# Dilated attention: turning the probabilities by a product with a diagonal matrix of reciprocal sums instead of scaling and transposing them

## The chip, the cores and the metric

The kernel runs on one core of one Trainium2 chip. The metric is the device time of one execution in microseconds. The times shown are medians of several executions; the profile is one execution taken by the hardware profiler, whose own clock starts at the first instruction and ends at the last (the span).

## The reference, cut to what matters

The program is a deep block: two layers of feed-forward network, mixer, feed-forward network with layer norms, then two more layers of a second kind of mixer. Only the mixer of the second layer matters here, dilated attention over 512 positions with three groups (window 128 at stride 1, 512 at stride 4, 2048 at stride 16), 16 heads of 64 each:

```python
scores = einsum(q, k) * E ** -0.5 + bias          # bias: minus slope times distance
scores = where(valid, scores, MASK_VALUE)
lse = logsumexp(scores, axis=-1)
p = exp(scores - lse[..., None])
o = einsum(p, v)                                  # per group
...
wts = softmax(stack(lses), axis=0)                # over the three groups
o = sum(wts[..., None] * stack(outs), axis=0)
return o.reshape(B, S, ATTN_WIDTH) @ w_out
```

A softmax over groups, weighted by their log-sums, is one softmax over the keys of all three groups. So the kernel puts the scores of the three groups side by side (512 + 128 + 128 columns for 128 queries), takes one minimum, one exponential, one sum and one reciprocal per query and head.

## The kernel before, in words

The stages run one after another: start, feed-forward, pooling mixer, two feed-forwards, **dilated attention**, feed-forward, two mixers of the second kind, end. Every engine has its own program; they meet in semaphores (`s["..."]`). Activations lie feature by position, 8 tiles of 128 x 512.

SP loads weights in chunks, GpSimd (POOL in the profile) splits each chunk into a high and a low part (`pool_weights`, two operations at L337 and L339 of up to 2048 columns per partition), and TensorE (PE) multiplies with both (L358, L989).

The attention stage (`pe_attn`, `act_attn`, `dve_attn`) treats the 16 heads in four **quads** of four. For each quad come nine weight chunks for q, k and v of the three groups (18 half chunks), then eight **pairs** `i`. A pair is two heads (`hh` = 0, 1) and one residue `r` of the query position, that is 128 queries. Per pair the engines do, in the order in which their instructions are issued:

- **TensorE**, iteration i of a quad: `pe_attn_turn(i-1, 0)`, `pe_attn_turn(i-1, 1)`, `pe_attn_scores(i+1)` and `pe_attn_out(i-1)`, below T0, T1, S and O. A turn transposes the probabilities of one head, six blocks of 128 x 128 (four of the far group at L861, two of the near groups at L867), into PSUM. S is ten score products (L848): six of 512 columns and four of 128. O is twelve products of turned probabilities with values (L887). In iteration 8 there is no S, and in the first three quads a half chunk of the next quad (24 matmuls of 512 columns, L358) stands ahead of the last turn.
- **VectorE** (DVE), iteration i: far scores of head 0 (L912), reciprocal (L934) and scaling (L935) of head 1 of pair i-1, near scores of both heads (L921), far scores of head 1 (L912), two minima (L928), reciprocal and scaling of head 0 of pair i. After pair 5 a low part of the output is split off (L1033).
- **ScalarE** (ACT), iteration i: three copies of the turned probabilities from PSUM to `at_pt` (L895), two exponentials with the sum as by-product (L902). After pair 5 also the high part of the output.

The waits around the change: T0 and T1 wait for `normed`; T0 also for `pt_copied` of the pair before; a scaling waits for `probs`; the exponential of head `hh` waits for `t_done`, because it overwrites `at_pr`, which the turns read; S waits for `sc_ready` of the pair before (its scores taken out of PSUM); O waits for `pt_copied`; the first far scores of a pair wait for `scored`.

`nc.tensor.transpose(out, x, identity)` is a matrix instruction in transpose mode, with `x` as the stationary operand and the identity as the moving one. `nc.tensor.matmul(out, x, d)` computes x transposed times d.

Of the kernel before, what the change touches and what calls it, by code (L numbers as in the profile page):

```python
# [20 lines left out]
F32 = mybir.dt.float32  # L21
# [4 lines left out]
P = 128  # L26
T = 512
# [186 lines left out]
class Kernel:  # L214
# [45 lines left out]
    def sb(self, name, shape, dt=F32, ctx=None):  # L260
        return (ctx or self.ctx).enter_context(self.nc.sbuf_tensor(name, shape, dt))
# [542 lines left out]
    def memory_attn(self, own):  # L804
        sb = self.sb

        self.at_qk0 = sb("at_qk0", [P, 2, 2, T], F32R, own)
        self.at_qk0_l = sb("at_qk0_l", [P, 2, 2, T], F32R, own)
        self.at_q = sb("at_q", [P, 2, 2, T], F32, own)
        self.at_k = sb("at_k", [P, 2, 2, T], F32, own)  # L810
        self.at_v = sb("at_v", [P, 3, 4, 256], F32, own)
        self.dist0 = (self.sq, sb("dist0", [P, 2, T], F32, own))
        self.dist12 = sb("dist12", [P, 2, P], F32, own)
        self.at_oh = sb("at_oh", [P, KT, T], F32R, own)
        self.at_ol = sb("at_ol", [P, KT, T], F32R, own)
        self.at_bias = self.stats[:].rearrange("p a (b t) -> p (a b) t", b=2)
        self.at_sc, self.at_pr = (sb(n, [P, 2, T + 2 * P], F32, own) for n in ("at_sc", "at_pr"))
        self.at_pt = sb("at_pt", [P, 3, T], F32, own)
        self.at_nb, self.at_den, self.at_rd = (sb(n, [P, 2, 2], F32, own) for n in ("at_nb", "at_den", "at_rd"))

# [32 lines left out]
    def pe_attn_turn(self, pe, st, i, hh):  # L853
        nc, s, ps = self.nc, self.s, self.ps
        pe.wait_ge(s["normed"].sem, st.at("normed", 2 * i + hh + 1))
        if i and hh == 0:
            pe.wait_ge(s["pt_copied"].sem, st.at("pt_copied", 3 * i))

        def far():
            for j in range(4):  # L860
                mm = nc.tensor.transpose(ps[:, self.TURNED + 2 * hh, j * P:(j + 1) * P], self.at_pr[:, hh, j * P:(j + 1) * P], self.identity[:])  # L861
            s["t_done"].up(mm)

        def near():
            for g in range(2):
                at = hh * 2 * P + g * P
                mm = nc.tensor.transpose(ps[:, self.TURNED + 1, at:at + P], self.at_pr[:, hh, T + g * P:T + (g + 1) * P], self.identity[:])  # L867
            if hh:
                s["t_done"].up(mm)
        for step in ((near, far) if hh else (far, near)):  # L870
            step()
# [58 lines left out]
    def dve_attn_norm(self, dve, st, i, hh):  # L930
        nc, s = self.nc, self.s
        dve.wait_ge(s["probs"].sem, st.at("probs", 2 * i + hh + 1))
        rd, pr = self.at_rd[:, i % 2, hh:hh + 1], self.at_pr[:, hh]
        self.dve_then(dve, nc.vector.reciprocal(rd, self.at_den[:, i % 2, hh:hh + 1]))  # L934
        s["normed"].up(nc.vector.tensor_scalar(pr, pr, rd, None, ALU.mult))  # L935

    @staticmethod
    def by_residue(ap):
# [1412 lines left out]
```

## Time and profile before

| | |
|---|---|
| median of 3 runs | 3788.59 us (3788.31 to 3789.31) |
| the profiled execution's own time | 3787.25 us |
| its span, first to last instruction | 3785.4 us |
| TensorE busy | 3440.3 us, 91% |
| VectorE busy | 1737.8 us, 46% |
| ScalarE busy | 798.0 us, 21% |
| GpSimd busy | 2200.1 us, 58% |
| pairs of the attention stage | from about 1485 to 2006 us of the span, in four stretches of some 53 us |

How to read it: the shares are averages over stages with different limits. The pairs are four stretches of 1/18 of the span together, and the change touches nothing outside them; what matters is the order of events in them, which the rows below show.

### The profile page before, as it was taken

To read this page: it belongs to the slowest core of one execution; us is meant where nothing else is said; L and a number is where in the kernel's file an instruction comes from. 1 tells how busy PE (TensorE), PEld (TensorE's weight loads), DVE (VectorE), ACT (ScalarE), POOL (GpSimd) and SP (SyncE) were. 2 spreads that over 40 slices of the span, in tenths; PEclk is the share of its full clock that TensorE was granted. 3 is DMA by queue.
4 is the path that set the end of the run, shared out by engine and by line. 5 is a ranking of instruction groups with operands and counts; after the bars stand their busy time and mean duration, and the time that the engine had idled before them with its cause. 6 is when DMAs were issued, how large, how long until landed. Compare 5 with 4: busy or idle time off the path is not lost.

```text
span 3785.4 us, 42681 instructions
## 1 busy us (share of the span) xinstructions
PE 3440.3 (91%) x16956; PEld 2739.8 (72%) x16956; DVE 1737.8 (46%) x2017; ACT 798.0 (21%) x1345; POOL 2200.1 (58%) x558
## 2 busy tenths in 40 slices
PE   6999878999899979989897999868999987899997
PEld 5887656888688858778775888646678765667875
DVE  6772574222422242351536222365667525566742
ACT  1000212110211022231323110031322212132321
POOL 6776555777577746436353777635445663445564
PEclk9999989999899989999998999979999998999998
DMA  5553222323223222112121232212222221222221
GB/s 179 177 177 107 82 67 67 96 90 98 72 89 98 92 78 89 45 56 81 42 78 45 78 100 95 89 55 67 62 63 66 77 91 56 62 56 67 68 81 64
DMA packets 321300, 312.56 MB, mean 83 GB/s; under 512 B 11376, under 2 KB 303888, under 8 KB 320784
## 3 DMA queue, kind: packets, MB, share of 16 engines
q1 hardware_dynamic: 303840, 277.91, 23.7%
q10 hardware_dynamic: 17328, 32.80, 2.5%
q8 instruction: 94, 1.54, 0.2%
q14 instruction: 38, 0.31, 0.0%
HBM read 308.57 MB, written 2.10 MB: 82 GB/s over the span
## 4 chain that ended last, share of the span: by engine, by line
PE 74%; DVE 15%; ACT 5%; issue 4%; DMA 2%; ACTq 0%; DVEq 0%
PE ps L358 48%; PE ps L1229 12%; PE ps L989 4%; DVE sq L1110 2%; PE ps L1271 2%; PE ps L463 1%; DMA ada_raw<-in_ada_w 1%; ACT x L494 1%; PE ps L1796 1%; ACT xh L500 1%; DVE at_sc L912 1%; DVE score L1561 1%; DVE top L1560 1%; DVE d_pr L1650 1%; PE ps L1609 1%
## 5 line engine op out<-in xcount | busy, mean ns | idle before, releaser
L337 POOL TENSOR_TENSOR wh<-w_raw,zero 128x2048 fp32r<-128x2048 f32 (+2 forms) x277 | 952.4, 3438 | 1522.1 <-PE ps L358 1016.0
L339 POOL TENSOR_TENSOR wl<-w_raw,wh 128x2048 fp32r<-128x2048 f32 (+2 forms) x277 | 1247.6, 4504 | 21.7
L358 PE MATMUL ps<-xh,wh 128*128 128x512 f32 x2160 | 857.1, 397 | 101.7 <-DVE xl L536 48.0
L358 PE MATMUL ps<-xl,wh 128*128 128x512 f32 x2160 | 847.9, 393 | 0.0
L358 PE MATMUL ps<-xh,wl 128*128 128x512 f32 x2160 | 847.5, 392 | 0.0
L358 PEld LDWEIGHTS ps<-xh,wh 128*128 128x128 f32 x2160 | 409.3, 190 | 211.0 <-issue 91.9
L358 PEld LDWEIGHTS ps<-xh,wl 128*128 128x128 f32 x2160 | 409.7, 190 | 86.7
L358 PEld LDWEIGHTS ps<-xl,wh 128*128 128x128 f32 x2160 | 410.3, 190 | 83.0 <-issue 1.0
L1229 PE MATMUL ps<-xh,wh 128*128 128x512 f32 x688 | 294.0, 427 | 8.1 <-ACT stats L1371 6.4
L358 PE MATMUL ps<-hid_h,wh 128*128 128x512 f32 x704 | 279.7, 397 | 7.6 <-DVE mod L1125 7.6
L626 DVE TENSOR_TENSOR hp<-sg,ps 128x512 f32<-128x512 f32 x88 | 60.3, 685 | 481.2 <-PE ps L358 481.2
L358 PE MATMUL ps<-hid_l,wh 128*128 128x512 f32 x704 | 279.4, 397 | 0.0
L358 PE MATMUL ps<-hid_h,wl 128*128 128x512 f32 x704 | 279.4, 397 | 0.0
L1229 PE MATMUL ps<-xl,wh 128*128 128x512 f32 x688 | 274.4, 399 | 0.0
L1229 PE MATMUL ps<-xh,wl 128*128 128x512 f32 x688 | 274.2, 399 | 0.0
L629 DVE TENSOR_TENSOR hid_l<-hp,hid_h 128x512 f32 x88 | 190.7, 2167 | 87.7 <-ACT hid_h L611 87.7
L640 DVE SCALAR_TENSOR_TENSOR x<-x,ps 128x512 f32<-128x512 f32 x32 | 22.0, 686 | 378.6 <-PE ps L358 378.6
L1229 PEld LDWEIGHTS ps<-xh,wh 128*128 128x128 f32 x688 | 132.9, 193 | 61.6 <-issue 31.5
L472 ACT ACTIVATE squares<-x 128x512 f32<-128x512 f32 x64 | 37.8, 626 | 654.2 <-DVE x L514 634.0
L358 PEld LDWEIGHTS ps<-hid_h,wh 128*128 128x128 f32 x704 | 132.9, 189 | 39.9 <-issue 7.7
L611 ACT ACTIVATE hid_h<-hp 128x512 f32 x88 | 55.6, 632 | 494.4 <-DVE hp L626 494.4
L358 PEld LDWEIGHTS ps<-hid_l,wh 128*128 128x128 f32 x704 | 133.0, 189 | 32.2
(286 smaller groups left out, 5102.0 us busy)
## 6 DMA issues: line engine op xcount, KB each, us to landing
w_raw<-in_w_in SPq DMA_DIRECT2D x120, 512.0 KB, 4.1
w_raw<-in_ffn_w_gate SPq DMA_DIRECT2D x88, 512.0 KB, 4.6
w_raw<-in_ffn_w_up SPq DMA_DIRECT2D x88, 512.0 KB, 4.8
w_raw<-in_attn_w_qkv SPq DMA_DIRECT2D x72, 512.0 KB, 4.5
w_raw<-in_ffn_w_down SPq DMA_DIRECT2D x64, 512.0 KB, 3.6
ada_raw<-in_ada_w ACTq DMA_DIRECT2D x24, 512.0 KB, 5.5
stats<-in_ada_w ACTq DMA_DIRECT2D x24, 512.0 KB, 5.1
w_raw<-in_ffn_w_down SPq DMA_DIRECT2D x32, 384.0 KB, 4.1
```

The lines of the kernel that those rows point to most:

```text
L337: t = s["w_hi"].up(pool.tensor_tensor(hi, raw, self.zero[:, 0:1].to_broadcast([P, n]), ALU.subtract))
L339: s["w_lo"].up(pool.tensor_tensor(lo, raw, hi.bitcast(F32), ALU.subtract))
L358: mm = self.nc.tensor.matmul(out, a[:, slot, w], b(t), start=start and t == 0 and q == 0, stop=stop and t == k - 1 and q == 2)
L463: s["var_part"].up(self.nc.tensor.matmul(self.ps[:, bank], self.ones[:], self.pair_at(p)[:], start=p == 0, stop=p == PAIRS - 1))
L494: t = s["x_ready"].up(nc.scalar.activation(self.x[:, m], self.x[:, m], ACT.Identity, scale=self.ln[:, 0, u, m:m + 1], bias=self.ln[:, 1, u ...
L611: s["hid_hi"].up(nc.scalar.activation(self.hid_h[:, 2 * i + m], self.hp[:, m], ACT.Copy))
L626: t = s["hid"].up(nc.vector.tensor_tensor(self.hp[:, m], self.sg[:, m], self.ps[:, 2 + m], ALU.mult))
L629: s["hid_lo"].up(nc.vector.tensor_tensor(self.hid_l[:, 2 * i + m], self.hp[:, m], self.hid_h[:, 2 * i + m].bitcast(F32), ALU.subtract))
L989: mm = self.nc.tensor.matmul(out, x[t][:, r], b[:, slot, w], start=t == 0 and q == 0, stop=t == KT - 1 and q == 2)
L1110: ins = v.scalar_tensor_tensor(total, raw, c, total, ALU.mult, ALU.add)
L1229: mm = self.nc.tensor.matmul(out, a[:, slot, w], b(t), start=first and t == ks[0] and q == 0, stop=last and t == ks[-1] and q == 2)
L1271: mm = self.nc.tensor.matmul(out, x[t][:, r], b[:, c % 2, w], start=t == 0 and q == 0, stop=t == KT - 1 and q == 2)
```

## The change

The scaling pass over 768 columns of probabilities (L935) goes. In its place VectorE scales the 128 x 128 identity by the reciprocal sums, row by row, which gives a diagonal matrix in a new tile `at_dg`. The six transposes of each head become six ordinary float32 products of the unscaled probabilities with that matrix: entry (k, q) of such a product is p(q, k) times 1/sum(q), so turning and scaling are one operation. The calls, their waits and their order stay the same.

```diff
+        self.at_dg = sb("at_dg", [P, 2, P], F32, own)
 ...
         def far():
             for j in range(4):
-                mm = nc.tensor.transpose(ps[:, self.TURNED + 2 * hh, j * P:(j + 1) * P], self.at_pr[:, hh, j * P:(j + 1) * P], self.identity[:])
+                mm = nc.tensor.matmul(ps[:, self.TURNED + 2 * hh, j * P:(j + 1) * P], self.at_pr[:, hh, j * P:(j + 1) * P], self.at_dg[:, hh], start=True, stop=True)
             s["t_done"].up(mm)
 
         def near():
             for g in range(2):
                 at = hh * 2 * P + g * P
-                mm = nc.tensor.transpose(ps[:, self.TURNED + 1, at:at + P], self.at_pr[:, hh, T + g * P:T + (g + 1) * P], self.identity[:])
+                mm = nc.tensor.matmul(ps[:, self.TURNED + 1, at:at + P], self.at_pr[:, hh, T + g * P:T + (g + 1) * P], self.at_dg[:, hh], start=True, stop=True)
             if hh:
                 s["t_done"].up(mm)
 ...
     def dve_attn_norm(self, dve, st, i, hh):
         nc, s = self.nc, self.s
         dve.wait_ge(s["probs"].sem, st.at("probs", 2 * i + hh + 1))
-        rd, pr = self.at_rd[:, i % 2, hh:hh + 1], self.at_pr[:, hh]
+        rd = self.at_rd[:, i % 2, hh:hh + 1]
         self.dve_then(dve, nc.vector.reciprocal(rd, self.at_den[:, i % 2, hh:hh + 1]))
-        s["normed"].up(nc.vector.tensor_scalar(pr, pr, rd, None, ALU.mult))
+        s["normed"].up(nc.vector.tensor_scalar(self.at_dg[:, hh], self.identity[:], rd, None, ALU.mult))
```

## Rows read from the trace of the kernel before

**Rows 1.** The page, the chain of work that ended last, by engine.

```profile
PE 74%; DVE 15%; ACT 5%; issue 4%; DMA 2%; ACTq 0%; DVEq 0%
```

**Rows 2.** Windows: length; busy (x) of PE, PEld, DVE, ACT, POOL; PEclk; DMA.

```profile
1671.49:1677.02 5.53, 4.64 (x53) 3.76 (x51) 5.19 (x10) 3.63 (x7) 0.00 (x0) 1.00 0.01 3
1655.50:1660.20 4.70, 4.65 (x28) 3.95 (x30) 4.39 (x7) 3.14 (x6) 0.00 (x0) 0.50 0.71 227
```

**Rows 3.** Timeline of VectorE, one pair of quad 2: start, length, operation, [idle before].

```profile
1670.29 0.62 DVE L935 TENSOR_SCALAR at_pr<-at_pr,at_rd 128x768 f32<-128x768 f32 x1
1670.83 0.74 DVE L912 SCALAR_TENSOR_TENSOR at_sc<-sq,slopes,ps 128x512 f32<-128x512 f32 x1
...
1672.81 0.74 DVE L912 SCALAR_TENSOR_TENSOR at_sc<-sq,slopes,ps 128x512 f32<-128x512 f32 x1
1673.58 1.81 DVE L928 TENSOR_REDUCE at_nb<-at_sc 128x1 f32<-128x768 f32 x2
1675.63 0.16 DVE L934 RECIPROCAL at_rd<-at_den 128x1 f32<-128x1 f32 x1 [0.24 <-ACT at_pr L902]
```

**Rows 4.** Timeline of TensorE in the same pair: first rows of T0, T1 and S.

```profile
1671.06 0.66 PE L861 MATMUL ps<-identity,at_pr 128*128 128x128 f32 x4
...
1672.35 0.44 PE L867 MATMUL ps<-identity,at_pr 128*128 128x128 f32 x2 [0.42 <-DVE at_pr L935]
...
1673.70 0.47 PE L848 MATMUL ps<-at_qk 64*128 64x512 f32 x1 [0.47 <-DVE at_sc L912]
```

**Rows 5.** Timeline of TensorE early in quad 2, one iteration in which it waits for nothing.

```profile
1661.34 0.66 PE L861 MATMUL ps<-identity,at_pr 128*128 128x128 f32 x4
...
1662.27 0.60 PE L861 MATMUL ps<-identity,at_pr 128*128 128x128 f32 x4
1662.80 0.50 PE L848 MATMUL ps<-at_qk 64*128 64x512 f32 x1
...
1664.27 1.53 PE L887 MATMUL ps<-at_pt,at_v 128*64 128x128 f32 x24
1665.73 0.44 PE L861 MATMUL ps<-identity,at_pr 128*128 128x128 f32 x2
```

**Rows 6.** VectorE scaling, lines of L935 and L1050: count, shortest/median/longest ns, first and last start.

```profile
L935 DVE TENSOR_SCALAR at_pr<-at_pr,at_rd x64: 619/621/4021, 1495.4 to 2002.2; 128x768 f32<-128x768 f32 x64
```

```profile
L1050 DVE TENSOR_SCALAR stats<-dist,slopes x32: 285/288/4661, 1413.7 to 1884.8; 128x128 f32<-128x128 f32 x32
```

**Rows 7.** TensorE, lines of L861 (transposes) and L1877 (plain products of another stage).

```profile
L861 PE MATMUL ps<-identity,at_pr x256: 270/273/474, 1496.4 to 2003.5; 128*128 128x128 f32 x128
```

```profile
L1877 PE MATMUL ps<-sd,gv x64: 271/275/275, 2911.1 to 3644.9; 128*128 128x128 f32 x64
```

**Rows 8.** Timeline of TensorE in the second kind of mixer.

```profile
2913.02 0.61 PE L1877 MATMUL ps<-sd,gv 128*128 128x128 f32 x4
```

**Rows 9.** Timeline of all engines, head of quad 2.

```profile
1650.38 4.70 POOL L339 TENSOR_TENSOR wl<-w_raw,wh 128x2048 fp32r<-128x2048 f32 x1
...
1651.48 4.01 DVE L935 TENSOR_SCALAR at_pr<-at_pr,at_rd 128x768 f32<-128x768 f32 x1
...
1655.55 0.69 PE L867 MATMUL ps<-identity,at_pr 128*128 128x128 f32 x2 [3.23 <-DVE at_pr L935]
```

**Rows 10.** Timeline of VectorE after pair 5 of quad 2.

```profile
1682.58 0.69 DVE L1033 TENSOR_TENSOR at_ol<-ps,at_oh 128x512 fp32r<-128x512 f32 x1 [0.58 <-ACT at_oh L1006]
```

**Rows 11.** Timeline of TensorE, end of quad 2: T0 of pair 6, O of pairs 6 and 7.

```profile
1688.93 0.65 PE L861 MATMUL ps<-identity,at_pr 128*128 128x128 f32 x4
...
1691.86 1.53 PE L887 MATMUL ps<-at_pt,at_v 128*64 128x128 f32 x24 [0.74 <-ACT at_pt L895]
...
1701.16 1.09 PE L887 MATMUL ps<-at_pt,at_v 128*64 128x128 f32 x16 [0.79 <-ACT at_pt L895]
```

**Rows 12.** Timeline, end of quad 4: T0 of pair 6, O of pair 7.

```profile
1996.53 0.66 PE L861 MATMUL ps<-identity,at_pr 128*128 128x128 f32 x4
...
2004.52 1.53 PE L887 MATMUL ps<-at_pt,at_v 128*64 128x128 f32 x24 [0.74 <-ACT at_pt L895]
```

## The prediction

> **What bounds the kernel now.** I read the page first, for the chain that ended last: it is TensorE's for the most part [rows 1], and the attention pairs are one place where that is not so. Then the timelines of the pairs, engine by engine, in a stretch without GpSimd or DMA traffic, and last the single lines for prices.
>
> In the steady part one pair follows another every 5.53 us, from one reciprocal of head 1 to the next, at the full clock of 2.4 GHz (PEclk 1.00), and VectorE is busy for 5.19 of them [rows 2]. Its one gap is 0.24 us, in which the reciprocal of head 0 waits for the exponential [rows 3]. TensorE waits twice in the same pair: T1 for the scaling of head 1, 0.42 us, and S for the far scores of head 1, 0.47 us [rows 4]. So VectorE, with the short ScalarE step in its loop, sets the pace. But TensorE is not far behind: early in a quad, where it has a backlog, one iteration takes 1.46 us for T0 and T1 (1661.34 to 1662.80), 1.47 for S and 1.46 for O (1664.27 to 1665.73), 4.39 us in all [rows 5]. The reader should see both numbers, 5.54 and 4.39: the change takes from the first and adds to the second.
>
> At the head of a quad something else holds: the scaling of head 1 of the first pair takes 4.01 us instead of 0.62, because it started inside a 4.70 us operation of GpSimd (1650.38 to 1655.08) and ended 0.41 us after it; T1 waited 3.23 us for it [rows 9]. In that gap the granted clock had fallen to 0.50, that is 1.2 GHz, and it stayed there over the whole of 1655.5 to 1660.2 although TensorE was busy for 4.65 of those 4.70 us [rows 2].
>
> **Change, VectorE's part.** Removed per head: a pass over 768 columns, 0.62 us long (median 621 ns), after which the next operation starts 0.54 us later [rows 3, 6]. Added: the same operation on 128 columns of an SBUF tile; L1050 is just that, 288 ns [rows 6]. So each head gives VectorE 0.33 us and each pair 0.67: its loop could turn in 5.54 - 0.67 = 4.87 us. At the head of a quad the short operation still can't start before GpSimd is through (the longest L1050 took 4661 ns [rows 6]); only the 0.41 us behind GpSimd's end shrinks, to about 0.08, so T1 starts 0.33 us earlier, at about 1655.2.
>
> **Change, TensorE's part.** A transpose is one matrix instruction: 64 heads x 4 at L861 give x256 records. A plain float32 product is two: L1877 issues 32 of them (two mixers, four heads, four blocks) and has x64 records of the same length, 271 to 275 ns [rows 7]. The step from one record to the next is what occupies the engine. For four transposes in a row it is (0.60 - 0.27)/3 = 0.11 us [rows 5]; for two plain products of 128 x 128 by 128 columns, four records, it is (0.61 - 0.275)/3 = 0.11 us as well [rows 8]. So a turned block costs 0.11 us now and 0.22 after. Bounds: 0.11 if the product with the diagonal were as cheap as a transpose, for which no row speaks; 0.23 if each pair of records lost a little to the doubled weight loads. I take 0.22, from the operation of the same shape and type. Twelve blocks per pair: T0 and T1 grow by 1.32 us, from 1.46 to 2.78, and TensorE's iteration from 4.39 to 5.71 us.
>
> The Trainium skill (TensorE: Matmul & The Clock Gate, Terms, row "xbus") says that transpose mode is four times faster for FP32. The trace shows twice, not four times; by the page, a product would cost 0.44 us against the transpose's 0.11. It stands as a rival below, and speaks in the same direction as my sum.
>
> **Who sets the pace then.** 5.71 is above 4.87, so TensorE becomes the bound if nothing makes it wait. From the start of an S: the last turned block is out about then; the copy and the step into the next operation take some 0.6 to 0.7 us (0.74 from the end of T1 to O, which waits for that copy [rows 11]), so the exponential of head 0 starts at S + 0.6. From the start of the minima to the reciprocal are 2.05 us [rows 3], of which the first minimum is about 0.95, so exponential to reciprocal is 1.07; then 0.2 for the reciprocal, 0.29 for the new scaling, 0.05 for the signal: the diagonal of head 0 is ready at S + 2.2. TensorE comes to T0 at S + 1.47 + 1.46 = 2.93. It does not wait; the slack is 0.7 us. Head 1: now T1 starts 1.52 us after the far scores of head 0 (1670.83 to 1672.35 [rows 3, 4]), then 1.19, which is S + 3.3 against T1's turn at S + 4.25, slack 1.0. Only after pair 5 is the slack used up: VectorE idles 0.58 us and spends 0.69 on the low part of the output [rows 10], 1.27 us, and the exponentials it waits behind come no earlier, which adds the 0.33 that the scaling gave: 1.6 - 1.0 = 0.6 us of wait.
>
> **The sum, per quad.** Old times from quad 2.
> - Head: T1, S and O of the first pair run at 1.2 GHz, 1655.55 to 1661.34 [rows 9, 5]. New: 0.66 us (full clock) more work, less the half of 0.33 that the earlier start is worth at half clock. The time of the clock's return is taken as it was, before the end of O, so added work counts at full clock: +0.5.
> - Five iterations from T0 of pair 1 to T0 of pair 6: 1688.93 - 1661.34 = 27.59 [rows 5, 11]. New 5 x 5.71 + 0.6 = 29.15: +1.56.
> - Pair 6, where no S stands between turn and output: T0 to O was 2.93 us (1688.93 to 1691.86 [rows 11]), with a wait for the scaling in it. New: 23 steps of 0.11, 0.27 for the last to end, 0.74 to O, 0.04: 3.58. +0.65.
> - Pair 7, in quads 1 to 3: a half chunk stands before its turn and covers all of VectorE's work, so the twelve longer blocks show in full before O (1701.16 [rows 11]) and behind it in the next quad: 12 x 0.11 = +1.32.
>
> That is 4.0 us a quad, 12.1 for three. In quad 4 there is no half chunk: T0 of pair 6 to O of pair 7 was 7.99 us [rows 12], and is 3.58 + 1.46 + 3.58 = 8.62, so +0.63 in place of the last two terms: 2.7. Together **+14.8 us**. What VectorE gains, 64 x 0.33 = 21 us, becomes idle time. Outside these stretches nothing changes: weights arrive ahead of need, and the new tile moves nothing that an engine's time depends on. Against the profiled execution: 3787.25 + 14.8 = 3802.1; the median of the runs is 1.3 us above that execution, so **3803 us**.
>
> **Rivals.**
> - *The clock comes back earlier.* The first turn of a quad now occupies TensorE about twice as long before the gap, and the gap shrinks from 3.23 us to some 1.6. If the clock is then at 2.4 GHz from T1 on, T1, S and O take 1.37 + 1.47 + 1.46 = 4.30 us from 1655.2, so T0 of pair 1 is at 1659.5 instead of 1661.9: 2.35 us less per quad, 9.4 in all, +5.4 in total, 3794 us. For it: the clock fell in a gap. Against: it stayed at 0.50 through 4.65 us of dense work [rows 2]. Chance 0.13. Beside it, the Trainium skill (TensorE: Matmul & The Clock Gate, Part 4: PE-mode transpose) says that transposes don't count as busy for the clock as products do; that rule would favour this rival, and this trace neither shows nor excludes it, since the steady pairs mix both at PEclk 1.00.
> - *VectorE's relief decides (faster).* If a product cost what a transpose does, TensorE would keep its 4.39, the loop would turn in 4.87 and each quad would lose 0.33 at its head, 0.67 in four of its five iterations and 0.33 in pair 6, about 3.5 us: -14 us, 3775. TensorE's iteration equals the old 5.54 at (5.54 - 3.07)/12 = 0.206 us per block; with the ends of the quads counted, the line between -14 at 0.11 and +14.8 at 0.22 crosses zero at 0.165, and as it is bent, the point lies between that and 0.2. Against it: every float32 product here has two records. Chance 0.06, with other gains of that sign.
> - *A product costs four transposes,* 0.44 us. TensorE's iteration would be 3.07 + 12 x 0.44 = 8.35 us, and some 31 pairs would pay 2.64 more than in my forecast: +97, 3885 us. That is the page's "4x" taken at its word. Against it stand the records of L1877 at 0.11. Chance 0.02.
>
> **How the numbers follow.** Forecast 0.79, the rest as above. A block at 0.21 or 0.23 instead of 0.22 moves 29 to 31 pairs by 0.12 us: 3.6 us either way. The clock's dips differ by steps (any shift of the stages moves when they start and end): some 3 us either way. So the likeliest case spans 3797 to 3810, and the range takes in the first rival with a few us below it: 3790 to 3810. No change that can be measured here is within 0.2%, 7.6 us. The forecast is beyond that except at its low end, the first rival is within it: slower 0.77, same 0.16, faster 0.07.
>
> **What would show it.** In the changed profile: L861 with two records per block, x512, and L867 x256; the step between them 0.11 us; T0 and T1 together 2.78 us with no wait before T1 or S; 5.7 us from pair to pair; VectorE idle over 0.8 us per pair, waiting for the exponentials; L935 at 0.29 us except under GpSimd. Wrong would be: one record per block or another step; an exponential that waits long enough for the turns to hold up T0 too (then more than 5.71); PEclk 1.00 right after the head of a quad.

## The result

The changed kernel takes 3798.66 us (median of 10 runs, 3796.88 to 3803.64), the kernel before 3789.4 us (10 runs, 3786.51 to 3791.1). The ratio is 1.0028 with a 95% interval from 1.0018 to 1.0038: slower by 0.28%, some 10.6 us, between 7 and 14 (the two medians are 9.3 us apart). The forecast was 3803 with a range from 3790 to 3810, and slower.

The two profiled executions are further apart, 3801.57 against 3787.25 us. The attention stage, from the reciprocal of the layer norm before it to the one behind it (VectorE, 512 columns), is 694.75 us long before and 708.77 after: +14.0. The stage begins 4.1 us later in the changed kernel's execution and what comes behind it is 3.8 us shorter; both stretches run the same code in both kernels. From here on the attention stage of the profiled executions is the yardstick; it is one execution of each kernel, and the ratio of the timed executions is put beside it where the two disagree. The page of the changed kernel, its busy times and its chain by engine, to be held against [rows 1] and the table:

```profile
PE 3479.7 (92%) x17340; PEld 2787.6 (73%) x17340; DVE 1713.8 (45%) x2017; ACT 799.0 (21%) x1345; POOL 2197.6 (58%) x558
PE 77%; DVE 14%; ACT 4%; issue 3%; DMA 2%; ACTq 0%; DVEq 0%
```

TensorE has 384 matmul records more (16956 before) and 39 us more work; VectorE has 24 us less. The single lines of the scaling and of the products answer to [rows 6] and [rows 7]:

```profile
L936 DVE TENSOR_SCALAR at_dg<-identity,at_rd x64: 285/287/3826, 1499.5 to 2019.9; 128x128 f32<-128x128 f32 x64
```

```profile
L862 PE MATMUL ps<-at_dg,at_pr x512: 271/276/423, 1500.1 to 2022.0; 128*128 128x128 f32 x171
```

The diagonal takes 287 ns where the scaling took 621; the far blocks have 512 records for 256 products. Now the timeline of TensorE over one pair in the steady part of quad 2, against [rows 4] and [rows 5]:

```profile
1675.27 1.16 PE L862 MATMUL ps<-at_dg,at_pr 128*128 128x128 f32 x8
1676.26 1.06 PE L868 MATMUL ps<-at_dg,at_pr 128*128 128x128 f32 x8
1677.15 1.06 PE L862 MATMUL ps<-at_dg,at_pr 128*128 128x128 f32 x8
...
1679.61 1.53 PE L888 MATMUL ps<-at_pt,at_v 128*64 128x128 f32 x24
1681.07 0.38 PE L862 MATMUL ps<-at_dg,at_pr 128*128 128x128 f32 x1
```

No row has an idle time noted (it would stand in brackets). The two turns run as one piece, S follows at 1678.14, and the next T0 starts 5.80 us after this one. The window of that pair says the same, against [rows 2] (length; busy of PE, PEld, DVE, ACT, POOL; PEclk; DMA):

```profile
1675.27:1681.07 5.80, 5.80 (x64) 5.19 (x62) 4.53 (x10) 3.62 (x7) 0.00 (x0) 1.00 0.00 0
```

TensorE is busy for all of it, VectorE for 4.53 us instead of 5.19. And the timeline of VectorE, against [rows 3]:

```profile
1676.82 1.81 DVE L929 TENSOR_REDUCE at_nb<-at_sc 128x1 f32<-128x768 f32 x2
1679.79 0.17 DVE L935 RECIPROCAL at_rd<-at_den 128x1 f32<-128x1 f32 x1 [1.16 <-ACT at_pr L903]
1679.99 0.29 DVE L936 TENSOR_SCALAR at_dg<-identity,at_rd 128x128 f32<-128x128 f32 x1
```

What VectorE gained is waiting: 1.16 us ahead of the reciprocal where it was 0.24. The timeline of ScalarE shows what the exponential comes behind, the third copy, which itself waits for the turn:

```profile
1678.25 0.60 ACT L896 ACTIVATE at_pt<-ps 128x512 f32<-128x512 f32 x1 [0.30 <-PE ps L862]
1678.74 0.93 ACT L903 ACTIVATE at_pr<-at_sc,at_nb 128x768 f32<-128x768 f32 x1
```

### The profile page after: what moved, and what is told of

The parts are those of the page before. It is cut to its first block, busy times and chain, and to the rows that moved or that the text cites. A ratio compares the mean times of both kernels' runs of the same rounds, so it can differ in the third digit from the quotient of the medians.

```text
span 3799.8 us, 43449 instructions
## 1 busy us (share of the span) xinstructions
PE 3479.7 (92%) x17340; PEld 2787.6 (73%) x17340; DVE 1713.8 (45%) x2017; ACT 799.0 (21%) x1345; POOL 2197.6 (58%) x558
## 4 chain that ended last, share of the span: by engine, by line
PE 77%; DVE 14%; ACT 4%; issue 3%; DMA 2%; ACTq 0%; DVEq 0%
PE ps L358 48%; PE ps L1230 12%; PE ps L990 4%; PE ps L1272 2%; DVE sq L1111 2%; PE ps L862 2%; PE ps L463 2%; DMA ada_raw<-in_ada_w 1%; PE ps L888 1%; PE ps L849 1%; ACT x L494 1%; PE ps L1797 1%; DVE d_pr L1651 1%; DVE score L1562 1%; ACT xh L500 1%
## 5 line engine op out<-in xcount | busy, mean ns | idle before, releaser
L358 PE MATMUL ps<-xh,wh 128*128 128x512 f32 x2160 | 858.5, 397 | 101.2 <-DVE xl L536 47.4
L358 PE MATMUL ps<-xl,wh 128*128 128x512 f32 x2160 | 849.2, 393 | 0.0
L358 PE MATMUL ps<-xh,wl 128*128 128x512 f32 x2160 | 848.8, 393 | 0.0
L358 PEld LDWEIGHTS ps<-xh,wh 128*128 128x128 f32 x2160 | 409.9, 190 | 210.3 <-issue 91.7
L358 PEld LDWEIGHTS ps<-xh,wl 128*128 128x128 f32 x2160 | 410.4, 190 | 86.4
L358 PEld LDWEIGHTS ps<-xl,wh 128*128 128x128 f32 x2160 | 410.9, 190 | 82.6 <-issue 1.0
L358 PE MATMUL ps<-hid_h,wh 128*128 128x512 f32 x704 | 279.8, 397 | 7.4 <-DVE mod L1126 7.4
L358 PE MATMUL ps<-hid_l,wh 128*128 128x512 f32 x704 | 279.6, 397 | 0.0
L358 PE MATMUL ps<-hid_h,wl 128*128 128x512 f32 x704 | 279.5, 397 | 0.0
L358 PEld LDWEIGHTS ps<-hid_h,wh 128*128 128x128 f32 x704 | 133.0, 189 | 39.3 <-issue 7.4
L358 PEld LDWEIGHTS ps<-hid_l,wh 128*128 128x128 f32 x704 | 133.0, 189 | 32.0
```

Source lines behind the costliest of these rows:

```text
L358: mm = self.nc.tensor.matmul(out, a[:, slot, w], b(t), start=start and t == 0 and q == 0, stop=stop and t == k - 1 and q == 2)
```

## The experiments

All were compared with the kernel before on the same chip. "Stage" is the attention stage of the profiled execution, "head" the time from S of pair 1 to T0 of pair 1 in the four quads (it holds the wait for GpSimd and the low clock), "pair to pair" the distance of T0 to T0 in pairs 1 to 5, "pair 5" that from T0 of pair 5 to T0 of pair 6, "end" from T0 of pair 6 to the next quad's half chunk in quads 1 to 3. All are in us.

| kernel | head | pair to pair | pair 5 | end | stage | ratio (95%) |
|---|---|---|---|---|---|---|
| before | 14.5 to 15.3 | 4.39, 5.33 to 5.43, then 5.53 | 6.8 | 15.3 | 694.75 | 1 |
| changed | 14.4 to 15.7 | 5.80 | 6.4 | 17.2 | 708.77 | 1.0028 (1.0018 to 1.0038) |
| ident | 13.5 to 16.0 | 5.81 | 6.7 | 17.3 | 709.27 | 1.0034 (1.0021 to 1.0046) |
| twice | 14.9 to 16.0 | 5.70 | 6.6 | 17.1 | 709.99 | 1.0029 (1.0018 to 1.0041) |
| light | 13.6 to 15.0 | 4.39, 4.65, then 4.88 | 6.5, one 8.0 | 14.7 | 681.38 | 0.9963 (0.9949 to 0.9978) |
| f32r | 14.7 to 15.2 | 4.4 to 4.6, 4.65, then 4.87 | two 6.5, two 8 | 14.7 | 685.93 | 0.9968 (0.9956 to 0.9981) |
| split | 14.6 to 15.4 | 5.12, one 5.63 | 6.8 | 16.0 | 696.07 | 0.9994 (0.9985 to 1.0004) |
| half | 15.2 to 16.4 | 5.75 | 6.3 | 17.1, one 18.4 | 712.55 | one run |
| warm_prod | 13.3 | 5.55 | 6.8 | 15.3 | 693.10 | 0.9989 (0.9979 to 0.9998) |
| warm_turn | 13.3 | 5.54 | 6.8, one 8.4 | 15.3, one 14.7 | 693.58 | 0.9989 (0.9980 to 0.9999) |
| after_warm | 13.0 | 5.80 | 6.4 | 17.3 | 701.84 | 1.0020 (1.0011 to 1.0030) |
| f32r_warm | 12.8 | 4.88 | 8.0 to 8.8 | 14.7 to 15.2 | 684.79 | 0.9972 (0.9961 to 0.9982) |
| split_warm | 13.3 | 5.20 | 6.8 | 15.3 | 688.46 | 0.9981 (0.9971 to 0.9990) |
| f32r_warm2 | 12.8 | 4.88 | 6.5 | 14.6 | 676.03 | 0.9946 (0.9933 to 0.9960) |

A stage is read from one execution, a ratio from several. How far one execution can stray shows in the code that is the same in all fourteen kernels: the stage begins between 1373.2 and 1377.4 us, and what comes behind it takes between 1712.3 and 1717.7 us. So a difference of a few us between two stages counts only where its parts are seen in the timelines, and says little of the mean.

**TensorE's half alone (ident).** Products instead of transposes, the scaling pass kept:

```diff
-                mm = nc.tensor.transpose(ps[...], self.at_pr[:, hh, j * P:(j + 1) * P], self.identity[:])
+                mm = nc.tensor.matmul(ps[...], self.at_pr[:, hh, j * P:(j + 1) * P], self.identity[:], start=True, stop=True)
```

(the same for the near blocks)

> The kernel before, with its scaling pass over 768 columns kept, but each of the six turned blocks made by a plain float32 product with the identity instead of a transpose (nothing left out). Theory 1 (TensorE's occupation sets the pace: 24 records of 0.112 us for T0 and T1): from pair to pair 5.8 us as in the changed kernel, attention stage 14 to 17 us longer than before (the slack of 0.7 and 1.0 us takes up the 0.33 us of each longer scaling, except after pair 5). Theory 2 (the loop from T1 through copy, exponential and scaling back to T0 sets the pace, so VectorE's 0.67 us per pair count in full): 6.4 to 6.5 us from pair to pair, stage 30 us or more longer than before.

Measured: 5.81 us from pair to pair, stage +14.5. VectorE does 0.67 us more per pair than in the changed kernel and the pace is the same to 0.01 us. So theory 2 falls: VectorE's relief is worth nothing there, except after pair 5 (6.7 instead of 6.4).

**The same time on TensorE with another operation (twice).**

```diff
+                for _ in range(2):
-                mm = nc.tensor.transpose(...)
+                    mm = nc.tensor.transpose(...)
```

(the same for the near blocks)

> The kernel before with every transpose issued twice into the same place (same result, same scaling pass). Theory 1 (only the number of records on TensorE counts, 24 per pair at 0.112 us): 5.8 us from pair to pair, stage 14 to 17 us longer than before, as with products by the identity. Theory 3 (a product costs by its kind: longer weight loads, 190 against 141 ns, or full float32 work): doubled transposes cost less than products, pace 5.54 to 5.7 us, stage 3 to 10 us longer.

Measured: 5.70 us from pair to pair, stage +15.2. Timeline of TensorE, T0 and T1 of one pair:

```profile
1672.18 1.09 PE L862 MATMUL ps<-identity,at_pr 128*128 128x128 f32 x8
1673.11 1.04 PE L869 MATMUL ps<-identity,at_pr 128*128 128x128 f32 x8
1673.98 1.04 PE L862 MATMUL ps<-identity,at_pr 128*128 128x128 f32 x8
```

Eight doubled transposes step by (1.04 - 0.27)/7 = 0.110 us, eight records of products by (1.06 - 0.276)/7 = 0.112. So 0.1 of the 1.4 us that the turns grow by is the product's own (theory 3, in that size), the rest is the count of records.

**VectorE's half alone (light).** The scaling covers 128 of 768 columns; the other 640 columns of probabilities go on unnormalised:

```diff
-        s["normed"].up(nc.vector.tensor_scalar(pr, pr, rd, None, ALU.mult))
+        s["normed"].up(nc.vector.tensor_scalar(pr[:, 0:P], pr[:, 0:P], rd, None, ALU.mult))
```

> The kernel before with its transposes, but the scaling pass covers only the first 128 of 768 columns (left out: the scaling of the other 640, so their probabilities go on unnormalised). This is VectorE's relief alone. Theory 1: VectorE sets the pace before, so it falls by 2 x 0.33 to 4.87 us, TensorE's 4.39 stay below it; 3 to 4 us less per quad, stage 12 to 16 us shorter than before. If VectorE was not the bound (copies or exponentials instead): 5.2 to 5.5 us, stage 0 to 6 us shorter.

Measured: 4.88 us, stage -13.4, ratio 0.9963. The relief is real where TensorE has room; it is 0.65 us per pair, where I had worked out 0.67.

**Both halves, cheap products (f32r).** Probabilities and diagonal in float32r, so they are rounded further than before:

```diff
-        self.at_sc, self.at_pr = (sb(n, [P, 2, T + 2 * P], F32, own) for n in ("at_sc", "at_pr"))
-        self.at_dg = sb("at_dg", [P, 2, P], F32, own)
+        self.at_sc = sb("at_sc", [P, 2, T + 2 * P], F32, own)
+        self.at_pr = sb("at_pr", [P, 2, T + 2 * P], F32R, own)
+        self.at_dg = sb("at_dg", [P, 2, P], F32R, own)
```

> The changed kernel with the probabilities and the diagonal in float32r, so that a block is one record (less precise probabilities; nothing left out). Theory 1: if a record's step is 0.11 us whatever its type, T0 and T1 take 1.46 us again, the pace is VectorE's 4.87 us, stage 12 to 16 us shorter than before. If the doubled step of a float32 product is per pass and not per record, a float32r block could cost less than 0.11, with the same pace, since VectorE is then the bound. If float32r writes slow the exponential or the diagonal, 5.0 us or more.

Measured: 4.87 us, stage -8.8, ratio 0.9968. One record per block, at the transposes' step:

```profile
1672.07 0.66 PE L863 MATMUL ps<-at_dg,at_pr 128*128 128x128 f32 x4
1672.57 0.61 PE L869 MATMUL ps<-at_dg,at_pr 128*128 128x128 f32 x4
1673.01 0.61 PE L863 MATMUL ps<-at_dg,at_pr 128*128 128x128 f32 x4
```

The stage is 3.2 us short of the expected 12 to 16, a miss (the timed executions, at -12.1 us by their ratio, are not). Two of the four quads took 7.9 and 8.1 us at pair 5, 3.0 us too much together; the runs with fillers below come back to it. The heads did not shorten either: 60.1 us in all against 59.3 before.

**One head each way (split).** Head 0 with a diagonal and products, head 1 scaled and transposed.

```diff
+        dst, src = (self.at_pr[:, 1], self.at_pr[:, 1]) if hh else (self.at_dg[:, 0], self.identity[:])
+        s["normed"].up(nc.vector.tensor_scalar(dst, src, rd, None, ALU.mult))
```

> Balance: head 0 of each pair is turned by products with its diagonal matrix as in the changed kernel, head 1 is scaled in place and transposed as before (nothing left out). Theory 1: TensorE needs 4.39 + 0.66 + about 0.1 = 5.1 to 5.2 us per pair, VectorE 5.54 - 0.33 = 5.21, so 5.2 us from pair to pair, between the 4.87 of the relief alone and the 5.54 of before; at the ends of a quad the 0.66 us more of turning shows, so the stage is 1 to 5 us shorter than before. Rival (the loop of T1, copy, exponential, scaling is what counts): 5.5 us or more.

Measured: 5.12 us, and the window of one pair shows TensorE at its limit and VectorE at 4.79 us:

```profile
1669.43:1674.55 5.12, 5.12 (x59) 4.46 (x57) 4.79 (x9) 3.60 (x7) 0.00 (x0) 1.00 0.00 0
```

The stage is 1.3 us longer than before where I expected 1 to 5 less: a miss. The end of each quad pays 0.7 (16.0 against 15.3) and the first iteration is 5.12 where the kernel before had 4.39. The timed executions put this kernel some 2 us below the kernel before, an interval that takes in no difference (0.9985 to 1.0004), so which of the two is faster stays open.

**What a record is made of (half).** Only 64 columns of each diagonal stream; half of the queries of every block are left out.

```diff
-                mm = nc.tensor.matmul(ps[..., j * P:(j + 1) * P], ..., self.at_dg[:, hh], start=True, stop=True)
+                mm = nc.tensor.matmul(ps[..., j * P:j * P + 64], ..., self.at_dg[:, hh, 0:64], start=True, stop=True)
```

> The changed kernel with only the first 64 columns of each diagonal streamed (left out: half of the queries of every turned block, whose places in PSUM keep old values). It asks what a record of a float32 product of 128 columns is made of. If its 0.112 us is streaming time, a record falls to about 0.056 us and the pace to VectorE's 4.9 us; if it is the loading of 128 x 128 weights, the step stays 0.11 us and the pace 5.8 us.

Measured: 5.75 us from pair to pair. The timeline of TensorE:

```profile
1520.66 1.06 PE L868 MATMUL ps<-at_dg,at_pr 128*128 128x64 f32 x8
1521.55 1.06 PE L862 MATMUL ps<-at_dg,at_pr 128*128 128x64 f32 x8
```

With half the columns the step is still 0.112 us. What occupies TensorE in these turns is a fixed time per record, the same with 64 columns as with 128; that it is the loading of the next 128 x 128 weights is the explanation left, and was not tried by itself. It does not hold for any length: in the profile of the changed kernel matmuls of 256 columns (L990) follow each other every 0.12 us and those of 512 columns (L358) every 0.23.

**Work in TensorE's waits (warm_prod, warm_turn).** The kernel before, with fillers, that is work whose result nobody uses, at the head of each quad; below with products, in warm_turn with 22 and 28 transposes:

```diff
+        if i % QUAD_PAIRS == 0:
+            spare = ps[:, self.TURNED + 1, hh * 2 * P:hh * 2 * P + P]
+            for _ in range((11, 14)[hh]):
+                nc.tensor.matmul(spare, self.identity[:], self.identity[:], start=True, stop=True)
         pe.wait_ge(s["normed"].sem, st.at("normed", 2 * i + hh + 1))
```

> The kernel before with work for TensorE in its two waits at the head of each quad: 11 products identity x identity (float32, 128 columns) ahead of the first turn and 14 ahead of the second, into a place of PSUM that the turns overwrite (result unchanged). If the fall of the granted clock at the head comes from these waits, it stays at 1.00 and T1, S and O of the first pair take 3.65 instead of 5.2 to 5.8 us: 1.5 to 2.1 us less per quad, stage 6 to 9 us shorter. If the clock falls all the same, the fillers run at half clock and push the second turn back: stage 5 to 15 us longer.

> The same with 22 and 28 transposes of the identity, the same time on TensorE as the products. The Trainium skill (TensorE: Matmul & The Clock Gate, Part 4: PE-mode transpose) says that transposes do not count as busy for the clock: by it the clock falls as before and the fillers cost time (stage 5 to 15 us longer). If transposes count as products do: 6 to 9 us shorter, like the run with products.

Windows of the head of quad 1 (of quad 2 one stands in [rows 2]), before, then with products, then with transposes:

```profile
1500.70:1507.30 6.60, 6.14 (x44) 5.30 (x44) 6.26 (x12) 3.14 (x6) 0.00 (x0) 0.54 0.51 159
```

```profile
1500.00:1506.80 6.80, 5.53 (x61) 4.67 (x59) 6.49 (x8) 3.03 (x6) 2.04 (x1) 1.00 0.48 154
```

```profile
1500.00:1506.00 6.00, 4.66 (x53) 3.76 (x51) 5.69 (x8) 3.03 (x6) 0.96 (x1) 1.00 0.53 175
```

PEclk stays at 1.00 in all four heads and the head shrinks to 13.3 us. But the stage is only 1.7 and 1.2 us shorter, not 6 to 9: a miss, and the most useful one. In the kernel before, T0 of pair 1 came late and TensorE then made up for it with an iteration of 4.39 us, so T0 of pair 6 came 42.2 to 42.8 us after the S; with the fillers it comes after 42.3. VectorE's pace had covered the low clock. The timed executions gained more, 4.2 us (0.9989, that is between 0.8 and 8), and warm_turn the same; where the rest comes from no profile shows. Transposes kept the clock up as products did: the Trainium skill (TensorE: Matmul & The Clock Gate, Part 4: PE-mode transpose) says that they do not count as busy, and the runs with fillers do not bear it out.

**The fillers in the changed kernel (after_warm)**, 10 and 12 of them.

> The changed kernel with fillers for TensorE at the head of each quad (10 products of identities ahead of the first turn, 12 ahead of the second; result unchanged). In the kernel before the same fillers gave back only about 0.5 us a quad, although the first T1, S and O became 2 us shorter, because VectorE sets the pace there. If TensorE sets it in the changed kernel, the whole 1.4 to 2.7 us per quad must come back: stage 5 to 10 us shorter than in the changed kernel, pace still 5.8. If VectorE or the exponentials set it, again only some 2 us in all.

Measured: stage 701.84, 6.9 us shorter than in the changed kernel. Head 13.0 us in every quad, pace 5.80 as before. The window from T1 of pair 0 to the next T0, in quad 1:

```profile
1504.00:1508.10 4.10, 4.10 (x50) 3.49 (x48) 3.76 (x9) 3.12 (x6) 0.00 (x0) 1.00 0.83 256
```

The heads are 7.1 us shorter in all and the five iterations behind them take 29.6 us as they did, so in this execution the time at 1.2 GHz comes back in full where TensorE sets the pace. The timed executions do not show the difference: by their ratios the fillers take 0.08% (3 us) off the changed kernel and took 0.11% (4 us) off the kernel before, with intervals of 0.1% either way.

**The version that beats both.** At full precision: products only for head 0 of pairs 1 to 5, and the fillers of warm_prod (split_warm). The turn and the scaling ask this function which way to go:

```diff
+    def by_product(i, hh):
+        return hh == 0 and 1 <= i % QUAD_PAIRS <= 5
```

> Full precision, meant to be faster than both: products only for head 0 of pairs 1 to 5 of a quad, where VectorE is the bound; scaling and transposes elsewhere (both ends of the quad, where TensorE's time shows), and the fillers (11 and 14). Pace 5.12 us from T0 of pair 1 on instead of 5.53, after pair 5 6.8; no longer turn before the outputs of pairs 6 and 7. 1.5 to 2 us less per quad than before: stage 5 to 9 us shorter than before.

Measured: 5.20 us from pair to pair (5.12 expected), stage -6.3, ratio 0.9981. Then float32r with fillers of 10 and 14 (f32r_warm):

> The changed kernel with probabilities and diagonal in float32r (less precise probabilities) and the fillers (10 and 14). VectorE sets the pace at 4.87 us, so at the head the fillers give 0.5 to 1 us a quad; what they give beyond that would come from the missing dips of the clock later in the quad (2 of 4 quads of the run without fillers had one, 1.5 us each). Stage 2 to 7 us shorter than with float32r alone.

Measured: stage 684.79, only 1.1 us less than without: a miss. All four heads were at 12.8 us, but pair 5 now took 8.0 to 8.8 us in all four quads. In quad 1, TensorE waits there 1.34 us for the diagonal of head 1, and behind that wait the clock falls (the line of T1, then windows):

```profile
1530.82 0.44 PE L873 MATMUL ps<-at_dg,at_pr 128*128 128x128 f32 x2 [1.34 <-DVE at_dg L941]
```

```profile
1530.00:1532.00 2.00, 0.89 (x6) 0.74 (x6) 1.97 (x5) 0.70 (x2) 0.00 (x0) 0.89 0.02 4
1532.00:1534.00 2.00, 1.83 (x11) 1.73 (x13) 1.83 (x3) 1.34 (x4) 0.00 (x0) 0.50 0.00 0
1534.00:1537.00 3.00, 3.00 (x28) 2.77 (x26) 2.70 (x7) 0.99 (x3) 0.00 (x0) 0.50 0.00 0
```

So six more fillers went into that wait (f32r_warm2):

```diff
-        if i % QUAD_PAIRS == 0:
+        if i % QUAD_PAIRS in (0, 5):
-            for _ in range((10, 14)[hh]):
+            for _ in range(((10, 14) if i % QUAD_PAIRS == 0 else (0, 6))[hh]):
```

> The float32r kernel with fillers, and six more products of identities ahead of the second turn of pair 5, where TensorE waits 1.4 us (result otherwise unchanged; probabilities in float32r). In the run without them the granted clock fell to 0.50 there in all four quads and the iterations took 7.95 to 8.77 us instead of 6.48. If that wait is what costs the clock, pair 5 takes 6.5 us in every quad, 1.5 to 2.3 us less per quad, stage 6 to 9 us shorter than with the first fillers alone, about 677 us. If the clock falls later all the same (each iteration now leaves TensorE idle for 0.5 us of 4.9), the dip moves to another pair and the stage stays at 682 to 686 us.

Measured: pair 5 takes 6.48 us in all four quads, stage 676.03 (677 was expected), and 3768.53 us against 3788.54: ratio 0.9946, interval 0.9933 to 0.9960. The attention stage as one window in each profile, before, changed and this one:

```profile
1373.17:2067.92 694.75, 616.99 (x4106) 522.87 (x4106) 291.43 (x388) 185.17 (x331) 330.06 (x80) 0.96 0.20 63
```

```profile
1377.28:2086.05 708.77, 656.82 (x4490) 569.31 (x4490) 270.24 (x388) 186.38 (x331) 329.20 (x80) 0.97 0.19 62
```

```profile
1373.95:2049.98 676.03, 635.01 (x4346) 547.46 (x4346) 270.30 (x388) 183.36 (x331) 329.24 (x80) 0.98 0.20 65
```

## Why the prediction was right, step by step

**Direction and mechanism.** Right, and shown by taking the change apart. The pace of the pairs went from VectorE to TensorE; TensorE's half alone gives the whole loss (+14.5 of +14.0), VectorE's half alone would have given -13.4.

**The price of a block.** 0.22 us as forecast: 512 and 256 records, step 0.112 us. The Trainium skill (TensorE: Matmul & The Clock Gate, Terms) calls transpose mode four times faster for FP32 and does not say than what; against the plain products of this kernel the ratio is two. The run with half the columns says why the ratio here is one of records: each takes its 0.11 us with 64 columns as with 128.

**TensorE's iteration: 5.71 forecast, 5.80 measured.** The term T0 and T1 was mis-sized, 2.78 against 2.87 us (1675.27 to 1678.14). Of the 0.09, 24 steps of 0.112 instead of 0.110 are 0.05; the rest sits in the first records of the piece.

**No wait before T0 and T1, 0.6 us after pair 5.** Right. In the steady rows above nothing waits; pair 5 takes 6.39, which is 0.59 more than the others. VectorE idles 1.27 us per pair (over 0.8 forecast), and the diagonal of head 0 is ready 2.14 us after the start of S (1678.14 to 1680.28), where the forecast had 2.2.

**The sum by its terms, over all four quads:**

| term | forecast | measured |
|---|---|---|
| heads | 4 x 0.5 = +2.0 | +0.5, -0.4, -0.2, -0.1: -0.2 |
| five iterations | 4 x 1.56 = +6.2 | 2.0, 2.0, 2.0, 1.9: +7.9 |
| ends, quads 1 to 3 and quad 4 | 3 x 1.97 + 0.63 = +6.5 | 2.0, 2.0, 2.0, 0.7: +6.7 |
| sum | +14.8 | +14.3 |

The iterations came out 1.7 us dearer, by the 0.09 above, and the heads 2.2 us cheaper. That the sum is right to 0.5 us is in part luck: these two errors cancel. It is also the sum of one pair of executions; the timed ones differ by 10.6 us. The head was sized for a clock that comes back when it had come back before. It did so in quad 1:

```profile
1504.70:1509.50 4.80, 4.77 (x25) 4.39 (x26) 3.26 (x6) 2.40 (x5) 0.00 (x0) 0.50 0.68 218
```

In quad 2 of the kernel before, the clock had not fallen in the wait between T0 and T1, as the prediction says, but before it: T0 already ran at 0.50 (its first four transposes took 1.11 us, in the steady part 0.66), behind a wait of 2.75 us.

```profile
1650.77 1.11 PE L861 MATMUL ps<-identity,at_pr 128*128 128x128 f32 x4 [2.75 <-DVE at_pr L935]
```

```profile
1650.77:1652.30 1.53, 1.53 (x6) 1.14 (x6) 1.50 (x3) 0.38 (x1) 1.53 (x1) 0.50 0.00 0
```

In quad 2 of the changed kernel the clock was at 1.00 through the whole first turn and the wait behind it, fell only when T1 ran, and was back within the same iteration:

```profile
1659.00:1663.50 4.50, 1.58 (x12) 1.39 (x12) 4.46 (x4) 0.60 (x1) 4.42 (x1) 1.00 0.00 0
1663.50:1667.30 3.80, 3.75 (x23) 3.37 (x25) 3.15 (x5) 2.22 (x5) 0.00 (x0) 0.63 0.75 233
```

Quads 3 and 4 have heads as short as quad 2's (14.5 and 14.4 us, against 15.7 in quad 1). So the first rival came true in part, in three of four quads: the low clock cost less than forecast. Its condition, 2.4 GHz from T1 on, was met in none of them, and T1's wait was 2.1 to 3.0 us, not the 1.6 that the rival had. In ident it was met: in quad 3 the clock was at 0.50 under T0 and at 1.00 under T1, S and O, and the head took 13.5 us. The head of a TensorE-bound quad lies anywhere between these 13.5 us (ident, quads 3 and 4) and 16.0 (ident, quad 1), by when the clock happens to fall; what sets that moment stays open. The windows of ident, quad 3, are those of T0, of T1, and of S and O:

```profile
1817.23:1819.00 1.77, 1.77 (x8) 1.77 (x9) 1.74 (x3) 0.00 (x0) 1.77 (x1) 0.50 0.00 0
1821.20:1823.55 2.35, 1.53 (x12) 1.42 (x13) 2.31 (x4) 0.60 (x1) 0.34 (x1) 1.00 0.34 72
1823.55:1826.40 2.85, 2.85 (x39) 2.44 (x38) 2.58 (x5) 2.53 (x5) 0.00 (x0) 1.00 0.89 309
```

That the ten timed executions (3796.88 to 3803.64) and their smaller mean loss of 10.6 us come from the same scatter is likely, but only argued: nine of them have no timeline. The mean granted clock, which is kept for each, is 0.956 or 0.957 in the four that took over 3801 us and 0.957 to 0.959 in the other six.

**What the sum did not say.** In the profiled executions over a third of the loss is not the products' longer time as such. With fillers in both kernels, where the clock never falls at a head, the stage goes from 693.10 to 701.84, +8.7 us instead of +14.0. The other 5.3 us are stretches at 1.2 GHz that VectorE's slower pace used to cover, and that TensorE, once it sets the pace, shows in full. The forecast had them right in size, inside the term of the five iterations (the old 4.39 us was TensorE catching up; 5.71 in its place is 1.32 us a quad, 5.3 in four), but did not name them. The timed executions do not bear this share out: by their ratios the change costs 0.28% without fillers and 0.31% (1.0020 against 0.9989) with them. How much of the mean loss is low clock stays open.

**The faster rival** fell with its premise (two records per product), and f32r shows that its pace was well priced: with one record per block it is 4.87 us, as worked out. Its total of -14 us was not met there: the stage gave -8.8, by the two slow iterations at pair 5 and the heads. VectorE's relief alone gave -13.4 us (light), but by other terms: heads -2.6 where the rival had -1.3, iterations -7.9 (one slow pair 5 in them) where it had -10.7, ends -2.8 where it had -1.3.

## What to carry to other kernels

Before trading a pass on one engine for dearer operations on another, write down both engines' time per iteration: the gain is capped by the distance to the second one, here 5.53 down to 4.39, and 1.4 us on the one side overran 0.67 on the other. Price a small matrix product by its records and their step, not by its columns: here, with blocks of 128 x 128, a float32 product has two records where a transpose or a float32r product has one. And look for TensorE's waits even where another engine sets the pace, as VectorE does in f32r_warm: filling one wait of 1.3 us in each of four quads was worth 8.8 us of the stage, and the ratio went from 0.9972 to 0.9946, because of what the lower clock costs in the work behind it.

## What the runs showed of the hardware that was not expected

- The step from record to record in 128 x 128 turns is 0.110 us for transposes, 0.112 for records of float32 products, about 0.11 for float32r, and 0.112 with 64 columns instead of 128: up to 128 columns a fixed time per record.
- A kernel with VectorE relieved can lose the clock: in light, f32r and f32r_warm an iteration of 7.9 to 8.8 us follows TensorE's wait at pair 5 in one, two and four of four quads, with PEclk 0.50 over its windows of 3 us in f32r_warm (1534 to 1537) and light (1683 to 1686). The kernel before waits longer at the same place (1.7 us) and took 6.8 us in all four, but warm_turn, with the same wait, had one of 8.4. So the wait alone does not decide it, and why the clock fell in some and not in others is open; that filling the wait removed it was shown (6.48 us in all four quads of f32r_warm2).
- Fillers that are transposes kept PEclk at 1.00 through all four heads, as well as products did (warm_turn, warm_prod).
